# First block, both layers: the output projection's last half and the memory attention, by token tile

## The reference, cut to what matters

```
y = even_mixer(rms_norm(x, g[0]))  or  diff_mixer(...)     # ends with  o @ w_out   (1024 x 1024)
x = x + rms_norm(y, g[1])
q = (rms_norm(x, g[2]) @ wq) in 4 heads of 64              # wq 1024 x 256
k, v = mem_n @ wk, mem_n @ wv                              # 256 memory tokens, 4 heads
s = q k^T / 8 ; p = softmax(s) ; o = p v                   # all 256 memory tokens, no mask
x = x + rms_norm(o @ wo, g[3])                             # wo 256 x 1024
x = x + rms_norm(swiglu(rms_norm(x, g[4]), wg, wu, wd), g[5])
```

## Time and profile before

| | us |
|---|---|
| median of three runs | 2119.77 |
| span of the profiled execution | 2117.2 |
| TensorE busy with matmuls | 2033.5 (96%) |
| VectorE, ScalarE, GpSimd busy | 1252.6, 1043.3, 146.9 |
| mean granted clock of TensorE | 0.978 |

### The profile page before, as it was taken

One profiled execution on the slowest core, in us unless ns is written; L12 is line 12 of the kernel. 1 busy time (PEld: TensorE's weight loads), 2 busy tenths in 40 slices (PEclk: granted clock), 3 DMA queues, 4 the chain that ended last, 5 costly groups with the idle time before them and its releaser, 6 DMA issues.

```text
span 2117.2 us, 26909 instructions
## 1 busy us (share of the span) xinstructions
PE 2033.5 (96%) x9948; PEld 1675.8 (79%) x9948; DVE 1252.6 (59%) x1869; ACT 1043.3 (49%) x1680; POOL 146.9 (7%) x146
## 2 busy tenths in 40 slices
PE   7998899999879999999999999999999999999999
PEld 7775678887768888888778788888888877878887
DVE  5546654566765456545666865546554685775544
ACT  5545554455564445344556555435434556555443
POOL 0000000000010000000312200000000222120000
PEclk9987999999999999999999999999999999999999
DMA  8430365554236555555562545655555553435652
GB/s 289 125 112 11 128 205 185 193 188 153 67 118 199 182 191 175 192 181 178 153 202 88 179 139 179 193 184 180 193 185 188 170 184 119 159 121 179 196 181 100
DMA packets 247673, 346.13 MB, mean 163 GB/s; under 512 B 26164, under 2 KB 180088, under 8 KB 247544
## 3 DMA queue, kind: packets, MB, share of 16 engines
q1 hardware_dynamic: 246712, 342.92, 50.1%
q0 software_dynamic: 544, 1.29, 0.3%
q10 hardware_dynamic: 288, 0.21, 0.0%
HBM read 343.32 MB, written 2.33 MB: 163 GB/s over the span
## 4 chain that ended last, share of the span: by engine, by line
PE 88%; DVE 6%; ACT 3%; issue 2%; POOL 1%; DMA 0%; DVEq 0%; ACTq 0%; POOLq 0%
PE bank L666 26%; PE bank L668 26%; PE bank L667 26%; PE bank L942 2%; DVE w_lo L495 2%; PE bank L1070 1%; PE bank L1262 1%; PE bank L601 1%; ACT w_hi L507 1%; PE bank L1120 1%; POOL gain L2390 1%; PE bank L2047 1%; PE bank L1402 1%; DVE probs L1055 1%; DVE gain L1089 0%
## 5 line engine op out<-in xcount | busy, mean ns | idle before, releaser
L495 DVE TENSOR_TENSOR w_lo<-raw,w_hi 128x2048 fp32r<-128x2048 f32 (+5 forms) x491 | 743.0, 1532 | 421.5 <-ACT w_hi L507 421.2
L666 PE MATMUL bank<-w_hi,h_hi 128*128 128x512 f32 (+3 forms) x1904 | 747.2, 392 | 17.1 <-DVE w_lo L495 7.9
L507 ACT CAST w_hi<-raw 128x2048 fp32r<-128x2048 f32 (+5 forms) x491 | 620.3, 1291 | 265.0 <-PE bank L668 263.5
L668 PE MATMUL bank<-w_hi,h_lo 128*128 128x512 f32 (+3 forms) x1904 | 733.2, 385 | 0.0
L667 PE MATMUL bank<-w_lo,h_hi 128*128 128x512 f32 (+3 forms) x1904 | 732.8, 385 | 0.0
L666 PEld LDWEIGHTS bank<-w_hi,h_hi 128*128 128x128 f32 x1904 | 361.5, 190 | 90.9 <-DVE w_lo L495 5.5
L668 PEld LDWEIGHTS bank<-w_hi,h_lo 128*128 128x128 f32 x1904 | 361.1, 190 | 69.6
L667 PEld LDWEIGHTS bank<-w_lo,h_hi 128*128 128x128 f32 x1904 | 361.9, 190 | 63.9
L666 PE MATMUL bank<-w_hi,ff_hi 128*128 128x512 f32 x528 | 206.3, 391 | 0.0
L668 PE MATMUL bank<-w_hi,ff_lo 128*128 128x512 f32 x528 | 205.6, 389 | 0.0
L667 PE MATMUL bank<-w_lo,ff_hi 128*128 128x512 f32 x528 | 205.5, 389 | 0.0
(11 more groups left out here) (299 smaller groups left out, 1643.0 us busy)
## 6 DMA issues: line engine op xcount, KB each, us to landing
raw<-in_ffn_w SPq DMA_DIRECT2D x176, 512.0 KB, 4.7
raw<-in_w_in SPq DMA_DIRECT2D x48, 1024.0 KB, 5.3
raw<-in_ffn_w SPq DMA_DIRECT2D x44, 1024.0 KB, 4.9
raw<-in_ffn_wg SPq DMA_DIRECT2D x44, 512.0 KB, 4.0
raw<-in_ffn_wu SPq DMA_DIRECT2D x44, 512.0 KB, 5.0
raw<-in_ffn_wd SPq DMA_DIRECT2D x22, 1024.0 KB, 4.8
raw<-in_od_w_in SPq DMA_DIRECT2D x12, 1024.0 KB, 5.2
raw<-in_w_out SPq DMA_DIRECT2D x8, 1024.0 KB, 5.1
```

The source lines that it names most:

```text
L495: dve.tensor_tensor(lo_[:, cs], raw_[:, cs], hi[:, cs].bitcast(F32), ALU.subtract).then_inc(*dve_did.up())
L507: act.copy(hi[:, cs], raw_[:, cs]).then_inc(*act_did.up())
L666: pe.matmul(out, x_hi, u.hi[:, k, cols_], start=start, stop=False)
L668: return pe.matmul(out, x_lo, u.hi[:, k, cols_], start=False, stop=stop)
```

## The change

- `memory_attention` takes over the last half of the output projection. The mixers return it as a generator (`second_half`): both units are taken at once and run for tile 0, then for tile 1. Six of its eight steps are emitted, then the transposes and both splits of tile 0 of the next norm, then the last two steps.
- The general `attention` is replaced by a routine of its own that goes tile by tile. Tile 0's query transposes, scores and maxima are emitted between the transposes and the splits of tile 1 (`between`).
- `wq` gets a place of its own for its high part (`own_hi`, over `hT2`), so it uses none of the three high slots, and it may be split once `opened` is set. `wo` becomes one unit of 2048 elements. A unit's high slot is counted over the others alone (`before` is the unit three places ahead among them).
- `wo` is taken with `ahead=False`; there is no `prepare` in `memory_attention` any more, only three calls of `trickle` in gentle mode.
- The transposed probabilities lie in `z` and no longer in the spare gain; the transposes and the first split of the ffn's norm are emitted ahead of the last projection group.

```diff
-            for k0 in (0, KD // 2):
-                for _ in out_steps(acc, o_in, k0, attended["o"] if k0 else None, out_.leave):
-                    pass
-                if k0 == 0:
-                    memory_keys(0)
-            return out_
+            own_units[0].opened = attended["o"]
+            for _ in out_steps(acc, o_in, 0, None):
+                pass
+            memory_keys(0)
+            return second_half(acc, o_in, attended["o"], out_.leave)
...
+        def second_half(acc, h, ready, leave):
+            whole = [(c, take()) for c in (0, 512)]
+            for tt in range(TT):
+                for c, u in whole:
+                    yield from tile_steps(tt, h, KD // 2, u, KD, c, 512, acc[c],
+                                          (lambda k: ready) if tt == 0 and c == 0 else None, leave)
...
+        def may_part(n):
+            if n >= len(split_units) or split_units[n].landed is None:
                 return False
-            if not turn["gentle"] or of is units:
+            u = split_units[n]
+            if u.own:
+                return u.opened is not None
+            if u.before is None:
                 return True
-            return turn["steps"] - of[n - slots].at >= turn["lag"] and turn["steps"] - of[n].asked >= 4 * turn["lag"]
+            if u.before.used is None:
+                return False
+            if not turn["gentle"]:
+                return True
+            return turn["steps"] - u.before.at >= turn["lag"] and turn["steps"] - u.asked >= 4 * turn["lag"]
...
+            for _ in range(6):
+                next(products)
+            norm = begin_norm(x, col_of[("pre", l, 2)], rs[:, 0:2])
+            norm.turn()
+            norm.split(0)
+            norm.split(1)
+            for _ in products:
                 pass
...
+            ready = norm.rest()
+            wq = take(ahead=False)
...
+            queries(0)
+            ready.later(None, first_scores)
+            queries(1)
+            powers(0, 0)
+            powers(0, 1)
+            normalise(0, 0)
+            turn_query(1)
+            normalise(0, 1)
+            turn_probs(0, 0)
+            scores(1)
+            turn_probs(0, 1)
+            peak(1, 0)
+            peak(1, 1)
+            powers(1, 0)
+            powers(1, 1)
+            turn["gentle"] = True
+            trickle()
+            values(0)
+            normalise(1, 0)
+            normalise(1, 1)
+            turn_probs(1, 0)
+            turn_probs(1, 1)
...
+            turn["gentle"] = False
+            wo = take(ahead=False)
+            turn["gentle"] = True
+            project(0, 0)
+            trickle()
+            project(0, 512)
+            values(1)
+            trickle()
+            project(1, 0)
+            norm = begin_norm(x, col_of[("pre", l, 4)], rs[:, 0:2])
+            norm.turn()
+            norm.split(0)
+            project(1, 512)
+            for end in ends:
+                end()
+            ends.clear()
+            norm.split(1)
+            turn["gentle"] = False
+            attended["o"] = marks()
+            return norm.rest()
```

More of the change, by code:

```diff
@@ L242, in upto, with later @@
         return self.there[tt, (k - 1) // 2]
-    def later(self, places=None):
+    def later(self, places=None, between=None):
         if self.rest is not None:
-            self.rest(places)
+            self.rest(places, between)
             self.rest = None
@@ L260, in __init__ @@
         self.used = self.landed = None
-        self.whole = False
+        self.whole = self.own = False
+        self.opened = self.before = None
         self.at = self.asked = 0
@@ L326, in weight_stream @@
             units += half_units(a["od_w_out"][0], 0) + half_units(a["od_w_out"][0], KD // 2)
-        for name in ("ca_wq", "ca_wo"):
-            units += gemm_units(a[name][l], chunked(a[name].shape[2]))
+        units += gemm_units(a["ca_wq"][l], chunked(MEM_H * HD))
+        units[-1].own = True
+        src = a["ca_wo"][l].rearrange("(k p) n -> p k n", p=P)
+        units.append(Unit((MEM_H * HD // P, D), lambda v, src=src: [(v, src)]))
         units += ffn_units(a["ffn_wg"][l], a["ffn_wu"][l], a["ffn_wd"][l])
@@ L385, in program @@
         y_lo = sb("y_lo", [P, KD // 2, T], F32R, over=("hT2", KD // 2 * T))
+        own_hi = sb("own_hi", [P, SLOT], F32R, over=("hT2", 0))
         tmp = sb("tmp", [P, TT, D])
@@ L427, in program @@
         split_units = [u for u in units if u.split]
+        rounds = [u for u in split_units if not u.own]
+        for n, u in enumerate(rounds):
+            u.slot, u.before = n % HI_SLOTS, rounds[n - HI_SLOTS] if n >= HI_SLOTS else None
         banks = [Bank(ctx.enter_context(nc.psum_tensor(f"bank{i}", [P, 512], F32)), dve_did.now()) for i in range(8)]
@@ L430, in program @@
                 "normed": [pool_did.now()] * TT, "under way": iter(()), "gentle": False, "steps": 0, "lag": LAG}
+        own_units = [u for u in units if u.own]
         block = ctx.enter_context(nc.Block())
@@ L486, in part @@
             n = u.shape[0] * u.shape[1]
-            hi = w_hi[:, i % HI_SLOTS, 0:n]
+            hi = own_hi[:, 0:n] if u.own else w_hi[:, u.slot, 0:n]
             u.hi = hi.rearrange("p (a b) -> p a b", a=u.shape[0])
@@ L504, in _ @@
                     act.wait_ge(*u.landed)
-                    if i >= HI_SLOTS:
-                        act.wait_ge(*split_units[i - HI_SLOTS].used)
+                    if u.own:
+                        act.wait_ge(*u.opened.pe)
+                        act.wait_ge(*u.opened.act)
+                        act.wait_ge(*u.opened.dve)
+                        act.wait_ge(*u.opened.pool)
+                    elif u.before is not None:
+                        act.wait_ge(*u.before.used)
                     act.copy(hi[:, cs], raw_[:, cs]).then_inc(*act_did.up())
@@ L539, in prepare_steps @@
             load_more()
-            while (turn["parted"] < len(split_units) and split_units[turn["parted"]].landed is not None
-                   and free(split_units, turn["parted"], HI_SLOTS)):
+            while may_part(turn["parted"]):
                 turn["parted"] += 1
@@ L1452, in split_first, with later @@
                 split_half(0, half, first["full"], first["at"])
-            def later(places):
+            def later(places, between=None):
                 full, at_ = turn_tile(1, places)
+                if between is not None:
+                    rstd_tile(1)
+                    after = between()
                 for half in range(2):
                     split_half(1, half, full, at_)
-                rstd_tile(1)
+                    if between is not None:
+                        after(half)
+                if between is None:
+                    rstd_tile(1)
             def rest():
@@ L2305, in diff_mixer @@
                 fill()
+            own_units[1].opened = attended["o"]
             acc = out_banks()
@@ L2343, in program @@
         for l in range(DEPTH):
-            (even_mixer if l % 2 == 0 else diff_mixer)(load_gain(a["sandwich_g"][l, 1, :]))
-            memory_attention(l, load_gain(a["sandwich_g"][l, 3, :]))
-            ready = pre_norm(x, col_of[("pre", l, 4)], rs[:, 0:2])
+            products = (even_mixer if l % 2 == 0 else diff_mixer)(load_gain(a["sandwich_g"][l, 1, :]))
+            ready = memory_attention(l, products, load_gain(a["sandwich_g"][l, 3, :]))
             if l == 0:
```

193 lines of the change are left out of this document (168 added, 25 removed).

## The result

The changed kernel takes 2139.84 us, the median of 4 runs (2138.18 to 2141.67), where the kernel before took 2120.59 (2119.43 to 2123.1). The ratio is 1.0089, with an interval of 1.0077 to 1.01: 19 us slower. The forecast was 12.8 us slower, with a range that ended at 2137.

A forecast was written before the change was run, and what follows sets the result against it. TensorE, busy 2033.5 of 2117.2 us, was taken as the bound, so only its waits or clock count. Losses of 5.6 + 5.6 + 1.6 = 12.8 us on 2119.8 gave 2132.6, stated as 2132; range 2120 to 2137.

The forecast's parts named there:

- The ffn's first weights: At the ffn's start: all three casts emitted there, TensorE waits 7.4 us; layer 0 loses 5.6 us, restart included.
- The restart's clock: Behind the ffn's wait: restart at 1.2 GHz, eight matmuls at 0.43 instead of 0.23, 1.6 us more.
- `wq` in its own place: Layer 1, ahead of the projection's last half: a subtraction delays the low parts, 1.6 us lost (0 to 2.2).
- The whole middle brings 0.3 us: Layer 0, projection's last half to the end of `project`: done at 262.75 instead of 263.05.
- The paragraph on the clock: Memory attention: cutting the 3.05 us wait saves no clock; the sum stands without winning 4 us a layer.
- this wait of 2.3: Ahead of `project(1, 0)`: TensorE waits from 256.5 to 258.85, made by queue order.
- the 3 us wait at 246: Ahead of the transposes of tile 1's probabilities: TensorE waits from 246 to 249, made by queue order.
- The clock rule: TensorE: frequent short idle times between groups of matmuls can swing the clock as one long wait does.
- First unit split early: First ffn unit split inside the memory attention: 2117 to 2121, about 2114 with the second early too; chance 0.18.
- Clock holds: In the middle the clock holds, each layer ends 2 us earlier: 2128.5; chance 0.12.
- Worse: Clock stays at half from 240 to 258, 1.5 us a layer: 2136; chance 0.08.
- the middle takes as long as before within 2 us: Sign: from the projection's last half to the end of `project`, time as before within 2 us.

The follow-up runs named there:

- e1: Changed kernel with `wo` taken by a plain `take()`, so the first two ffn units are split there: 2123.59 us.
- e5: Kernel before with both units of `wo` taken with `ahead=False`, so all three ffn casts are emitted by the ffn: 2130.88 us.
- e6b: Changed kernel with 27 matmuls whose result nobody reads, put into bank 0 in the ffn's wait: 2134.46 us.
- e2: Changed kernel with layer 1's `wq` split only behind the low parts of the mixer's output: 2137.68 us.
- second profile: Profile of the changed kernel, unaltered, from its second measurement: 2138.92 us.
- e3: Changed kernel with banks 4 to 7 held back before the last transposes, so `project(0, 0)` meets a free one: 2137.64 us.
- e10: Changed kernel with e1, e2, e3 and e4 together, but the early ffn splits parted: one ahead of the `wo` product, one behind tile 1's values: 2113.98 us.
- e4: Changed kernel with tile 0's values rounded ahead of the last two of tile 1's four exponentials: 2137.62 us.
- three small mends: e2, e4 and e3, each alone in the changed kernel: 2137.68, 2137.62 and 2137.64 us.

## Why the prediction was right and wrong

*The ffn's first weights* (the term that carried the forecast). Right: no cast between the queries and the ffn, three in a row behind the tile's square, 7.0 us of waiting where 7.4 stood, in both layers, and `e1` and `e5` show the cause from both sides. `e5` gives 5 us a layer for it alone by its median (7.0 and 6.6 in its profiled execution, the slowest of the five), where 5.6 stood.

*The restart's clock.* Half, as said, but on 12 matmuls and not 8: from the first ffn matmul to the second unit 6.02 and 5.93 us in the first profile and 5.79 and 5.92 in the second (layers 0 and 1), against 2.75 + 1.1 + 1.6 = 5.45. An error of 0.3 to 0.6 a layer, which the shorter wait (7.0 for 7.4) nearly cancels. `e6b` puts the clock's price in that stretch at 2.3 to 2.4 a layer.

*`wq` in its own place.* Forecast 1.6, 1.40 in the row, 1.2 to 2.2 by `e2`. Right.

**The step that failed is "The whole middle brings 0.3 us", and in it the term for the clock: half clock on eight matmuls of `project(0, *)`, 1.6 us, and nowhere else.** From the start of the last half to the end of `project` the forecast had 262.75 - 216.66 = 46.1 us. The traces have (first ffn matmul, less the wait ahead of it, less the start) 273.27 - 7.01 - 216.35 = 49.9 and 638.67 - 7.01 - 583.00 = 48.7, and in the second profile 47.9 and 48.5. The kernel before has 46.4 in both layers. So the middle lost 1.5 to 3.5 us a layer instead of winning 0.3. Against the forecast that is 6.4 us in the first profile, of the 6.9 that its stretches are above the 12.8, and 4.3 of 4.4 in the second.

The stretch parts into idle time, busy time at full clock, and what the half clock adds (half of the time that TensorE worked at it). The first row is an estimate from the forecast's own figures, the others are from the traces; the work at full clock is 33 us in each.

| us, the middle of one layer | idle | added by half clock |
|---|---|---|
| forecast (46.1 less 33 less 1.6) | 11.5 | 1.6 |
| before, layers 0 and 1 | 9.1, 9.2 | 4.4, 4.2 |
| changed, first profile | 11.0, 11.4 | 5.8, 4.4 |
| changed, second profile | 10.9, 11.4 | 4.1, 4.2 |

The waits were forecast well in sum: 1.8 to 2.1 us more than before, where the forecast had some 2.3. The clock was not. It cost what it had cost before, and in layer 0 of the first profile 1.3 more; the forecast took 1.6 and so set some 2.7 us of regained clock against the new waits. That is how a loss of some 2 us came out as a win of 0.3. The paragraph on the clock said that the sum "already stands without that win" of 4 us; it held more than half of it. (My own sum has a slip beside it: eight matmuls at 0.2 more make 4.4 for `project(0, *)` and not 4.2.)

Where it shows in layer 0 of the first profile:

- Half clock on all 12 matmuls of `project(0, *)`, 5.42 us from 251.81 to 257.23, where I had 4.2. In the second profile it is 4.27, but tile 0's scores and a part of tile 1's queries were at half clock instead. They reach `project(1, 0)` after 44.4 and 44.05 us, where I had 42.2.
- `project(0, 0)` waits 0.78 us for its bank, which VectorE was still copying the last probabilities out of. I had followed the data of every step and not the banks. `e3` shows it.
- The clock fell once more behind the 2.11 us wait, 1.6 us for `project(1, *)` and the norm's transposes. I had left this wait of 2.3 without a price. In the second profile, and in layer 1 of both, it did not fall there.

The order of events was right within this stretch (the 3 us wait at 246 was 2.91, that of 2.3 was 2.11 and 2.44).

*The clock rule.* I held that cutting the long wait into pieces saves no clock. That was right: the middles of the two layers together spent 20.5 us at half clock before, and 23.9 and 20.5 in the two profiles of the changed kernel. By the Trainium skill (TensorE: Matmul & The Clock Gate, "A second HAM failure mode: psum-queue depth-cycling") short gaps between groups of matmuls can make the clock swing between its levels; the traces agree, with the fall at 236.1 us in the second profile behind gaps of 1.11 and 0.55. The mistake was not in the rule but in a sum that did not follow it. At the ffn, where the kernel before had no half clock, the late split adds 17.1 and 13.7 us of it over both layers, some 10 of them while each layer's twelve matmuls run.

*The rivals.* "First unit split early" was priced 2117 to 2121, and about 2114 with the second early as well. `e1` splits both, and it came out at 2123.6: the branch was right, its arithmetic too kind by the same middle (49.6 and 50.2 us there). That `e10` measured 2114.0 is no success of that figure, since it has three more edits and the splits placed apart. "Clock holds" failed in all the profiles. "Worse", at 0.08, named half clock from 240 to 258 at 1.5 us a layer; it was the nearest to what happened, still 4 us short, and deserved more, since the sum counted slow matmuls in one place only. Of the signs named ahead, the one that failed is that the middle takes as long as before within 2 us: it took up to 3.5 more.

What stays open: which part of the new waits the order by tile needs (`e3` and `e4` take away 1.7 us a layer of them); why the clock falls in one place in one execution and in another in the next; and how much of the three small mends' 1.2 to 2.2 us is the base's uncertainty.

## What to carry to other kernels

Where weights are split ahead of need, look for who emits the split and behind what on each in-order queue, before asking what an order of the matmuls gains: one argument was worth 16 us, one subtraction of 2.29 us in each layer 7, and the order by tile 3 to 5. Follow each step's bank as well as its data. And give the clock a term of its own, on both sides: take what half clock costs in the stretch before, here 4.2 to 4.4 us a layer, and let the sum regain it only where a trace shows why. Here waits of 0.5 to 2.9 us between groups of 1 to 3 us kept that cost where it was or raised it.

## What the runs showed of the hardware

Transposes follow the clock too: eight of 128x128 took 1.03 to 1.25 us at full clock and 1.91 to 1.94 at half. Matmuls that compute nothing hold the clock: 27 in 6.35 us gave the ffn a full-clock start, worth 2.3 to 2.4 us a layer, while 7 and 8 in the middle's waits took 6.8 us of half clock away over two layers and gained no time. With the same waits to 0.01 us until the first of them slowed down, two executions of one kernel had their half clock in different stretches (from 247.7 and 261.4 us, and from 236.1 and 249.7), and lost 9.6 and 7.4 us in layer 0.
